# Multiplying the merge gates with the branches' output gates inside the input projection

## The chip, the cores and the metric

The kernel runs on one NeuronCore of a Trainium2 chip. The metric is the device time of one launch in microseconds (us). The engines are named as the profile names them: PE is TensorE (PEld its weight loads), DVE VectorE, ACT ScalarE, POOL GpSimd, SP SyncE, which here only issues DMA transfers.

## What is computed

The network is an attention block of two layers over 1024 tokens of width 1024, and behind it one hybrid block. The change lies in the hybrid block. Cut to what matters there:

```python
proj = h @ w_in                                     # [1024, 14368]
(a_q, a_f, a_i, a_g, b_q, b_k, b_v, b_gk, b_g,
 c_qkv, c_a, c_b, c_g, merge) = jnp.split(proj, cuts, axis=-1)
...
gk  = b_gk @ gla_w_gk + gla_b_gk                    # from 16 columns of proj
y_a = rmsnorm(o_a, hgrn_onorm) * silu(a_g)          # each [1024, 1024]
y_b = rmsnorm(o_b, gla_onorm)  * silu(b_g)
y_c = rmsnorm(o_c, gdn_onorm)  * silu(c_g)
g = sigmoid(merge).reshape(..., 3, 1024)
y = g[:, :, 0] * y_a + g[:, :, 1] * y_b + g[:, :, 2] * y_c
x = x + rmsnorm(y @ w_out, ln_mix_post)
x = x + rmsnorm(square(relu(rmsnorm(x) @ w_up)) @ w_down, ln_mlp_post)
```

The kernel uses sigmoid(m) = (1 + tanh(m/2)) / 2. The factor 1/2 is folded into the head gains `onorm`, so a merge gate enters as 1 + tanh(m/2). Everything is float32.

## The kernel before

The hybrid block is a row of stages, each a block of its own with a barrier of all engines at its end. Four matter here.

**The input projection** is `seven_products`. It first computes one plain product, then the 32 narrow columns (16 of `b_gk`, 16 of `c_a` and `c_b`) into the SBUF tensor `low`, and then 13 groups, q = 0 to 12, of 1024 output columns each. A group is done with seven half-size products (i = 0 to 6) in place of eight. Each product has two units, u = 0 and 1, of 24 times 3 matmul passes over split operands; units are counted g = 0 to 13 within a group below (units 12 and 13 are product 6; "unit 14" is the next group's first, "unit 16" its third). For a unit ACT rounds half a weight block (`unit_hi`, line 900, into `p_th`), DVE forms the rest (`unit_lo`, line 1028, into `p_tl`), and PE waits for the latter. `th` and `tl` have two buffers, so unit g + 2 is prepared after PE has finished unit g. DVE also forms the sums of weight blocks T1 to T4 (lines 1033, 1038, 1042, 1046); T1 of the next group stands ahead of `unit_lo(14)`, T2 ahead of `unit_lo(15)`. The products 2, 4, 5 and 6 give the group's outputs, four tiles of 128 x 512 each: DVE adds PSUM to a partial sum into one of four slots of the ring `stg` (`joined`, lines 1059 and 1061), ACT applies a function in place (`activated`, line 911), in some groups POOL multiplies in place by a head gain (line 979), and SP stores the tile (line 719); `joined` waits until the slot's last store has landed. On ACT and DVE the order is written out: `unit_hi(g + 2)` and `unit_lo(g + 2)`, then the four tiles of `activated` or `joined`.

Groups 4, 8 and 9 are the output gates `b_g`, `c_g` and `a_g`: Silu on ACT, then the gain on POOL. Groups 10 to 12 are the three merge gates: Tanh on ACT, then the store. The result lies in `pn_dram`.

**The small projections** (`small_projections`) multiply `low` with two small matrices on PE right at the block's start. **The branches** (`gated_linear`, `gated_delta`) follow and write their normed outputs to `o_dram[0..2]`.

**The closing stage** (`closing`) merges. For each of eight row tiles SP loads three branches of three 128 x 1024 tiles: output gate `g`, merge gate `mg`, branch output `o`. DVE (`merge`, lines 3564 to 3573) computes (mg + 1) * g, times o, and sums over the branches into `y`; PE turns `y` (line 3322) and multiplies it with `w_out` (line 3327), in plain float32. A tile's loads go into one of two buffers, and SP issues tile t + 2 once `y` of tile t is ready.

Of the kernel before, what the change touches and what calls it, by code (L numbers as in the profile page):

```python
# [20 lines left out]
P = 128  # L21
# [576 lines left out]
def seven_products(C, x_in, first, groups, gains):  # L598
# [7 lines left out]
    with ExitStack() as st:  # L606
# [22 lines left out]
        sq = C.low  # L629
        ps = st.enter_context(nc.psum_tensor("p2_ps", [P, NB, CH], F32))  # L630
# [36 lines left out]
        s_gn = sem("gain_multiplied")  # L667
        block = st.enter_context(nc.Block())
# [10 lines left out]
        for g in groups:  # L679
            n_act.append(n_act[-1] + (16 if g["act"] else 0))  # L680
            n_gain.append(n_gain[-1] + (16 if g["gain"] is not None else 0))
# [9 lines left out]
        def _(sp):  # L691
# [17 lines left out]

            def store(q, i, j):  # L710
                n = out_n(q, i, j)
                k = n - PLAIN - 16 * q
                if groups[q]["gain"] is not None:
                    sp.wait_ge(s_gn, n_gain[q] + k + 1)
                elif groups[q]["act"]:
                    sp.wait_ge(s_act, n_act[q] + k + 1)
                else:
                    sp.wait_ge(s_C, ADDS * q + added[i] + (2 * j if i == 5 else j) + 1)
                sp.dma_start(where(q, i, j), stg[:, n % SG, :]).then_inc(s_st[n % SG], 16)

# [20 lines left out]
            for u in range(NB):  # L741
                store_plain(1, u)
            for q in range(NQ):
                for i, freed in ((2, ((1, 8), (3, 10))), (4, ((0, 12),)), (5, ((2, 14),)), (6, ())):
# [114 lines left out]
        def _(act):  # L859
# [48 lines left out]
            def activated(q, i, j):  # L908
                x = stg[:, out_n(q, i, j) % SG, :]
                act.wait_ge(s_C, ADDS * q + added[i] + (2 * j if i == 5 else j) + 1)  # L910
                act.activation(x, x, groups[q]["act"], scale=0.5 if groups[q]["act"] == ACT.Tanh else 1.0).then_inc(s_act, 1)
# [41 lines left out]
        def _(pool):  # L953
# [996 lines left out]
def small_projections(C):  # L1950
# [4 lines left out]
    with ExitStack() as st:  # L1955
# [8 lines left out]
        s_gD = sem("logits_taken_by_dve")  # L1964
        block = st.enter_context(nc.Block())

        @block.tensor
        def _(pe):
            for h in range(2):
# [1182 lines left out]
def closing(C, out):  # L3152
# [11 lines left out]
    br = [N_AG, N_BG, N_CG]  # L3164
    NJ = len(br)
# [6 lines left out]
    with ExitStack() as st:  # L3172
# [20 lines left out]
        o, g, mg = (lambda b, j, i=i: ogm[:, b, i, j, :] for i in range(3))  # L3193
# [459 lines left out]
def second_block(C, out, x_in):  # L3653
# [5 lines left out]
    with ExitStack() as s2:  # L3659
# [12 lines left out]
        with fresh_semaphores(nc):  # L3672
            with ExitStack() as s3:
                C.spare, C.low = spare, sb("low", [P, SEQ], F32, s3)
                C.onorm = [sb(f"onorm{j}", [P, D // h], F32, s3) for j, h in enumerate((A_HEADS, B_HEADS, C_HEADS))]
                w = ins["w_in_2"][0]
                pt, pn = C.pt_dram, C.pn_dram
                token = lambda a, c, act=None, gain=None: dict(w=w[:, a:a + D], out=pn[:, c:c + D], kind="token", act=act, gain=gain)
                silu = lambda j: dict(act=ACT.Silu, gain=C.onorm[j][:])
                channel = lambda a, r, act=None: dict(w=w[:, a:a + D], out=pt[r:r + D, :], kind="channel", act=act, gain=None)  # L3680
# [4 lines left out]
                               + [token(MERGE + D * i, N_M + D * i, ACT.Tanh) for i in range(3)],  # L3685
# [143 lines left out]
```

## Time and profile before

| | |
|---|---|
| time, median of 3 runs | 4582.42 us (4579.99 to 4585.22) |
| the profiled execution | 4588.66 us, span 4586.9 us |
| granted TensorE clock, mean | 0.965 of full speed |
| PE busy | 4186.2 us, 91% |
| DVE, ACT, POOL busy | 55%, 39%, 14% |
| the 13 groups of the projection | about 1805 to 2822 us of the span |
| small projections | 2825.0 to 2841 us |
| merge and its product | 3730.7 to 3873.5 us |

The span is the time from the first to the last instruction of the profiled execution; its own run took 1.8 us more than the span. Full speed of the clock (1.00) is 2.4 GHz, 0.50 is 1.2 GHz.

### The profile page before, as it was taken

How to read it: one execution, taken by the hardware profiler on the slowest of the kernel's cores; microseconds unless marked ns; L12 is line 12 of the kernel's file. 1: busy time of each engine (PE TensorE's matmuls, PEld its weight loads, DVE VectorE, ACT ScalarE, POOL GpSimd, SP SyncE). 2: the span in 40 equal slices, each digit the busy share in tenths (PEclk: the TensorE clock that was granted, in tenths of full speed). 3: DMA queues.
4: the chain of work that ended last, by engine and by line, in shares of the span. 5: the costliest groups of instructions: out<-in, count | busy, mean ns of one | idle time of the engine just before them, and what ended most of it. 6: DMA issues, size and time to landing. Idle time of an engine off the chain costs nothing. (4 is left out here: it accounts for less than half of the span.)

```text
span 4586.9 us, 66646 instructions
## 1 busy us (share of the span) xinstructions
PE 4186.2 (91%) x26765; PEld 3263.0 (71%) x26765; DVE 2513.5 (55%) x3323; ACT 1799.9 (39%) x3273; POOL 657.2 (14%) x759
## 2 busy tenths in 40 slices
PE   7999889889988979999999997788589979999999
PEld 1887667668756767888887785565388855888887
DVE  1413777651277756555656553787577756334333
ACT  0312456431145642222223333777566513423222
POOL 0200400020030010000102200776212101000000
PEclk9999999999999989999999998899799989999999
DMA  7434411134331131333333232112211056323322
GB/s 268 160 112 155 143 60 49 63 135 142 117 128 55 44 129 56 119 102 103 117 101 120 101 120 78 47 62 89 95 43 39 30 200 236 110 101 129 101 92 83
DMA packets 250802, 485.61 MB, mean 106 GB/s; under 512 B 33048, under 2 KB 73208, under 8 KB 250124
## 3 DMA queue, kind: packets, MB, share of 16 engines
q1 hardware_dynamic: 250512, 481.60, 30.4%
q8 instruction: 199, 3.26, 0.3%
q14 instruction: 91, 0.75, 0.1%
HBM read 360.42 MB, written 121.13 MB: 105 GB/s over the span
## 5 line engine op out<-in xcount | busy, mean ns | idle before, releaser
L1028 DVE TENSOR_TENSOR p_tl<-spare,p_th 128x1024 fp32r<-128x1024 f32 x156 | 199.4, 1279 | 359.4 <-ACT p_th L900 359.4
L900 ACT CAST p_th<-spare 128x1024 fp32r<-128x1024 f32 x156 | 163.5, 1049 | 566.7 <-PE p_ps L852 566.7
L316 PE MATMUL p_ps<-p_wh,hi 128*128 128x512 f32 x896 | 352.2, 393 | 5.7 <-DVE p_wl L484 5.7
L316 PE MATMUL p_ps<-p_wh,lo 128*128 128x512 f32 x896 | 350.2, 391 | 0.0
L316 PE MATMUL p_ps<-p_wl,hi 128*128 128x512 f32 x896 | 350.1, 391 | 0.0
L852 PE MATMUL p_ps<-p_th,p_xh 128*128 128x512 f32 x784 | 310.2, 396 | 2.0 <-DVE p_tl L1028 2.0
L852 PE MATMUL p_ps<-p_th,p_xl 128*128 128x512 f32 x784 | 309.9, 395 | 0.0
L852 PE MATMUL p_ps<-p_tl,p_xh 128*128 128x512 f32 x784 | 309.9, 395 | 0.0
L852 PE MATMUL p_ps<-p_xh,p_th 128*128 128x512 f32 x672 | 263.1, 391 | 1.0 <-DVE p_tl L1028 1.0
L852 PE MATMUL p_ps<-p_xh,p_tl 128*128 128x512 f32 x672 | 263.7, 392 | 0.0
L852 PE MATMUL p_ps<-p_xl,p_th 128*128 128x512 f32 x672 | 262.6, 391 | 0.0
L3594 DVE TENSOR_TENSOR z_wl<-spare,z_wh 128x2048 fp32r<-128x2048 f32 x62 | 142.1, 2293 | 182.1 <-ACT z_wh L3476 182.1
L484 DVE TENSOR_TENSOR p_wl<-p_raw,p_wh 128x2048 fp32r<-128x2048 f32 x40 | 91.5, 2292 | 242.1 <-ACT p_wh L408 242.1
L3345 PE MATMUL z_ps<-z_wh,z_uh 128*128 128x512 f32 x512 | 199.6, 390 | 1.8 <-ACT spare L3483 1.6
L3345 PE MATMUL z_ps<-z_hi,z_wh 128*128 128x512 f32 x512 | 200.0, 391 | 0.0
L3345 PE MATMUL z_ps<-z_hi,z_wl 128*128 128x512 f32 x512 | 199.2, 389 | 0.0
L3345 PE MATMUL z_ps<-z_wh,z_ul 128*128 128x512 f32 x512 | 199.2, 389 | 0.0
L3345 PE MATMUL z_ps<-z_wl,z_uh 128*128 128x512 f32 x512 | 199.2, 389 | 0.0
L3345 PE MATMUL z_ps<-z_lo,z_wh 128*128 128x512 f32 x512 | 199.2, 389 | 0.0
L316 PEld LDWEIGHTS p_ps<-p_wh,hi 128*128 128x128 f32 x896 | 169.3, 189 | 41.1 <-DVE p_wl L484 6.5
L316 PEld LDWEIGHTS p_ps<-p_wl,hi 128*128 128x128 f32 x896 | 169.4, 189 | 34.9
L316 PEld LDWEIGHTS p_ps<-p_wh,lo 128*128 128x128 f32 x896 | 169.1, 189 | 35.4
(422 smaller groups left out, 9902.8 us busy)
## 6 DMA issues: line engine op xcount, KB each, us to landing
spare<-w_in SPq DMA_DIRECT2D x56, 1024.0 KB, 5.6
p_raw<-w_in SPq DMA_DIRECT2D x40, 1024.0 KB, 5.9
pn_dram<-p_stg SPq DMA_DIRECT2D x128, 256.0 KB, 2.0
spare<-w_down SPq DMA_DIRECT2D x32, 1024.0 KB, 4.8
spare<-w_up SPq DMA_DIRECT2D x30, 1024.0 KB, 5.3
p_dram<-p_stg SPq DMA_DIRECT2D x112, 256.0 KB, 2.1
m_w<-w_mod SPq DMA_DIRECT2D x12, 2048.0 KB, 11.8
pt_dram<-p_stg SPq DMA_DIRECT2D x96, 256.0 KB, 2.2
```

Of the source, the lines that this page charges most:

```text
L316: mm = pe.matmul(ps[:, u, :], lhsT, rhs, start=(kk == 0 and q == 0), stop=(kk == KD - 1 and q == 2))
L484: dve.tensor_tensor(wl[:, kh], raw[:, kh], wh[:, kh], ALU.subtract).then_inc(s_wl[kh], 1)
L852: mm = pe.matmul(ps[:, bank + j, :], lhsT, rhs, start=(kk == 0 and e == 0), stop=(kk == KH - 1 and e == 2))
L900: act.copy(th[:, g % 2], (R11, T, R21, R12, R22, R11, R21)[i][:, 2 * u:2 * u + 2]).then_inc(s_hi, 1)
L1028: dve.tensor_tensor(tl[:, g % 2], (R11, T, R21, R12, R22, R11, R21)[i][:, 2 * u:2 * u + 2], th[:, g % 2], ALU.subtract).then_inc(s_lo, 1)
L3345: mm = pe.matmul(ps_ap, lhs[a], rhs[b], start=(start and q == 0), stop=(stop and q == 2))
L3594: dve.tensor_tensor(wl[:, b], raw(b, n), wh[:, b], ALU.subtract).then_inc(s_wl[b], 1)
```

## The change

The multiplication of the two gates moves from the closing stage into groups 10 to 12 of the projection, where the merge gate is made. There, ACT applies Tanh, drains, and adds 1 with a second instruction; POOL multiplies the tile by the output gate, which SP loads back from `pn_dram` (48 loads of 256 KB, three buffers, the first three ahead, each further one after the store of the tile three before it). The buffers are the two halves of `low` and one new tensor `gt`; so SP writes the 32 narrow rows of `low` to DRAM after the narrow product, and the small projections load them back before their first matmul. In the closing stage the load of `g` goes, with the instruction (mg + 1) * g.

```diff
+        gate = (C.low[:, 0:CH], C.low[:, CH:], gt[:])
...
+            def load_gate(m):
+                q, i, j = gated[m]
+                _, a, b = next(o for o in OUTS if o[0] == i)
+                from_q = groups[q]["gate_from"]
+                for x in range(SG):
+                    sp.wait_ge(s_st[x], 16 * ((PLAIN + 16 * (from_q + 1)) // SG))
+                sp.dma_start(gate[m % 3], groups[q]["gate"][(j + 4 * a) * P:(j + 4 * a + 1) * P, b * CH:(b + 1) * CH]).then_inc(s_gl[m % 3], 16)
...
                 sp.dma_start(where(q, i, j), stg[:, n % SG, :]).then_inc(s_st[n % SG], 16)
+                if groups[q]["gate"] is not None:
+                    m = gate_n(q) + k + 3
+                    if m < len(gated):
+                        load_gate(m)
...
+            sp.wait_ge(s_eA, 8 + 2)
+            sp.dma_start(C.low_dram, C.low[0:2 * RANK, :]).then_inc(s_low, 16)
...
-                act.activation(x, x, groups[q]["act"], scale=0.5 if groups[q]["act"] == ACT.Tanh else 1.0).then_inc(s_act, 1)
+                e = act.activation(x, x, groups[q]["act"], scale=0.5 if groups[q]["act"] == ACT.Tanh else 1.0)
+                if groups[q]["gate"] is not None:
+                    act.drain()
+                    e = act.activation(x, x, ACT.Copy, bias=1.0)
+                e.then_inc(s_act, 1)
...
+                elif groups[q]["gate"] is not None:
+                    for k in range(16):
+                        m = gate_n(q) + k
+                        pool.wait_ge(s_act, n_act[q] + k + 1)
+                        pool.wait_ge(s_gl[m % 3], 16 * (m // 3 + 1))
+                        x = stg[:, (PLAIN + k) % SG, :]
+                        pool.tensor_tensor(x, x, gate[m % 3], ALU.mult).then_inc(s_gn, 1)
...
+        @block.sync
+        def _(sp):
+            sp.dma_start(low, C.low_dram).then_inc(s_low, 16)
...
+            pe.wait_ge(s_low, 16)
...
                 for j in range(NJ):
-                    sp.dma_start(g(b, j), C.pn_dram[rows, br[j]:br[j] + D]).then_inc(s_in[j][b], 16)
-                    sp.dma_start(mg(b, j), C.pn_dram[rows, N_M + j * D:N_M + (j + 1) * D]).then_inc(s_in[j][b], 16)
+                    sp.dma_start(g(b, j), C.pn_dram[rows, N_M + j * D:N_M + (j + 1) * D]).then_inc(s_in[j][b], 16)
...
-                    dve.wait_ge(s_in[j][b], 48 * (t // 2 + 1))
-                    dve.scalar_tensor_tensor(g(b, j), mg(b, j), 1.0, g(b, j), ALU.add, ALU.mult)
-                    dve.drain()
+                    dve.wait_ge(s_in[j][b], 32 * (t // 2 + 1))
...
-                               + [token(MERGE + D * i, N_M + D * i, ACT.Tanh) for i in range(3)],
+                               + [dict(token(MERGE + D * i, N_M + D * i, ACT.Tanh), gate=pn[:, c:c + D], gate_from=f) for i, (c, f) in enumerate(((N_AG, 9), (N_BG, 4), (N_CG, 8)))],
```

On ACT, in groups 10 to 12, the four tiles of a product stand between two roundings of weight blocks. Before (the end of group 11's product 4 and what follows it):

```order
L900 CAST p_th<-spare 128x1024 x4
L911 ACTIVATE p_stg<-p_stg 128x512 x4
L900 CAST p_th<-spare 128x1024 x2
L911 ACTIVATE p_stg<-p_stg 128x512 x4
L900 CAST p_th<-spare 128x1024 x2
```

Now, one product of such a group (936 is Tanh, 939 adds 1, 925 is the rounding of a weight block):

```order
L925 CAST p_th<-spare 128x1024 x4
L936 ACTIVATE p_stg<-p_stg 128x512
L939 ACTIVATE p_stg<-p_stg 128x512
L936 ACTIVATE p_stg<-p_stg 128x512
L939 ACTIVATE p_stg<-p_stg 128x512
L936 ACTIVATE p_stg<-p_stg 128x512
L939 ACTIVATE p_stg<-p_stg 128x512
L936 ACTIVATE p_stg<-p_stg 128x512
L939 ACTIVATE p_stg<-p_stg 128x512
```

Eight instructions stand ahead of the next rounding in place of four. On SP, in the same groups, each store is now followed by a load of a gate, and the weight block of the next group stands behind four such pairs (`low` and `p_gt` are gate buffers, `spare` holds the weight blocks):

```order
L734 DMA pn_dram<-p_stg 128x512
L723 DMA low<-pn_dram 128x512
L734 DMA pn_dram<-p_stg 128x512
L723 DMA p_gt<-pn_dram 128x512
L734 DMA pn_dram<-p_stg 128x512
L723 DMA low<-pn_dram 128x512
L734 DMA pn_dram<-p_stg 128x512
L723 DMA low<-pn_dram 128x512
L711 DMA spare<-w_in 128x4x512
```

Before, the same place read:

```order
L719 DMA pn_dram<-p_stg 128x512 x4
L704 DMA spare<-w_in 128x4x512
```

## Rows read from the trace of the kernel before

**Rows 1.** The page, busy time by engine.

```profile
PE 4186.2 (91%) x26765; PEld 3263.0 (71%) x26765; DVE 2513.5 (55%) x3323; ACT 1799.9 (39%) x3273; POOL 657.2 (14%) x759
```

**Rows 2.** Stretches of the merge: PE, PEld, DVE, ACT, POOL busy, clock, DMA share, GB/s.

```profile
3730.00:3752.00 22.00, 2.31 (x9) 1.94 (x10) 12.25 (x10) 1.01 (x1) 0.00 (x0) 0.50 0.94 366
3752.00:3761.00 9.00, 9.00 (x20) 3.86 (x20) 7.35 (x6) 0.00 (x0) 0.00 (x0) 0.79 1.03 410
...
3776.00:3873.50 97.50, 97.50 (x284) 47.41 (x283) 76.42 (x87) 33.41 (x64) 13.11 (x30) 1.00 0.70 274
```

**Rows 3.** PE in order of time at the merge: start, us; idle before in brackets.

```profile
3748.50 1.97 PE L3322 MATMUL z_ps<-ident,z_y 128*128 128x128 f32 x8 [26.97 <-DVE z_y L3573]
3751.66 9.16 PE L3327 MATMUL z_ps<-spare,z_yT 128*128 128x512 f32 x16 [1.19 <-ACT z_yT L3437]
...
3775.27 1.04 PE L3322 MATMUL z_ps<-ident,z_y 128*128 128x128 f32 x8
```

**Rows 4.** SP in order of time, the first load of the merge.

```profile
3730.71 0.34 SPq L3256 DMA_DIRECT2D z_ogm<-pn_dram  x1
```

**Rows 5.** DVE in order of time, the merge of row tile 0 and its end.

```profile
3736.95 1.23 DVE L3564 SCALAR_TENSOR_TENSOR z_ogm<-z_ogm 128x1024 f32<-128x1024 f32 x1 [16.19 <-DMA z_ogm<-oa_dram]
...
3740.78 1.22 DVE L3564 SCALAR_TENSOR_TENSOR z_ogm<-z_ogm 128x1024 f32<-128x1024 f32 x1 [1.31 <-DMA z_ogm<-ob_dram]
...
3747.22 1.23 DVE L3573 TENSOR_TENSOR z_y<-z_y,z_ogm 128x1024 f32<-128x1024 f32 x1
```

**Rows 6.** DVE in order of time, group 11 going over to 12 (Tanh only).

```profile
2738.76 2.28 DVE L1033 TENSOR_TENSOR spare<-spare 128x2048 f32<-128x2048 f32 x1
2740.97 1.22 DVE L1028 TENSOR_TENSOR p_tl<-spare,p_th 128x1024 fp32r<-128x1024 f32 x1
...
2745.86 2.48 DVE L1059 TENSOR_TENSOR p_stg<-p_U,p_ps 128x512 f32<-128x512 f32 x4 [0.16 <-issue]
```

**Rows 7.** ACT in order of time, the same place.

```profile
2742.71 1.05 ACT L900 CAST p_th<-spare 128x1024 fp32r<-128x1024 f32 x1 [2.85 <-PE p_ps L852]
2746.59 2.42 ACT L911 ACTIVATE p_stg<-p_stg 128x512 f32<-128x512 f32 x4 [2.83 <-DVE p_stg L1059]
...
2753.91 1.05 ACT L900 CAST p_th<-p_T 128x1024 fp32r<-128x1024 f32 x1 [3.96 <-PE p_ps L852]
```

**Rows 8.** DVE in order of time, group 9 (Silu, then POOL).

```profile
2568.97 2.09 DVE L1028 TENSOR_TENSOR p_tl<-spare,p_th 128x1024 fp32r<-128x1024 f32 x1 [1.74 <-ACT p_th L900]
...
2583.25 2.30 DVE L1028 TENSOR_TENSOR p_tl<-spare,p_th 128x1024 fp32r<-128x1024 f32 x1
```

**Rows 9.** PE in order of time, group 9 going over to 10.

```profile
2585.61 0.50 PE L852 MATMUL p_ps<-p_th,p_xh 128*128 128x512 f32 x1 [0.95 <-DVE p_tl L1028]
```

**Rows 10.** POOL in order of time, group 9's product 4, first and fourth multiply.

```profile
2566.18 2.54 POOL L979 TENSOR_TENSOR p_stg<-p_stg,onorm 128x512 f32<-128x512 f32 x2 [16.37 <-ACT p_stg L911]
...
2569.93 2.28 POOL L979 TENSOR_TENSOR p_stg<-p_stg,onorm 128x512 f32<-128x512 f32 x1
```

**Rows 11.** ACT in order of time, a drain between two dependent instructions.

```profile
1695.40 1.14 ACT L881 ACTIVATE p_full<-p_ps,mix_scale 128x128 f32<-128x128 f32 x4 [2.95 <-PE p_ps L769]
1696.62 0.62 ACT L884 CAST p_xh<-p_full 128x512 fp32r<-128x512 f32 x1
```

**Rows 12.** ACT and then PE in order of time, end of the projection.

```profile
2813.09 0.63 ACT L911 ACTIVATE p_stg<-p_stg 128x512 f32<-128x512 f32 x1 [2.14 <-DVE p_stg L1059]
...
2821.83 0.63 ACT L911 ACTIVATE p_stg<-p_stg 128x512 f32<-128x512 f32 x1 [0.77 <-DVE p_stg L1059]
...
2825.03 7.16 PE L1974 MATMUL s_pg<-low,wg 16*128 16x512 f32 x8 [3.96 <-PEq L606]
```

**Rows 13.** DMA issues by line: count, KB each, median us to landing.

```profile
pn_dram<-p_stg SPq DMA_DIRECT2D x128, 256.0 KB, 2.0
...
a_mix<-mix_dram SPq DMA_DIRECT2D x18, 256.0 KB, 3.7
...
f_raw<-p_dram SPq DMA_DIRECT2D x2, 256.0 KB, 2.5
```

More of the change, by code:

```diff
@@ L629, in seven_products @@
         sq = C.low
+        gt = sb("gt", [P, CH])
+        gate = (C.low[:, 0:CH], C.low[:, CH:], gt[:])
         ps = st.enter_context(nc.psum_tensor("p2_ps", [P, NB, CH], F32))
@@ L667, in seven_products @@
         s_gn = sem("gain_multiplied")
+        s_low = sem("narrow_stored")
+        s_gl = [sem(f"gate_loaded{b}") for b in range(3)]
         block = st.enter_context(nc.Block())
@@ L680, in seven_products @@
             n_act.append(n_act[-1] + (16 if g["act"] else 0))
-            n_gain.append(n_gain[-1] + (16 if g["gain"] is not None else 0))
+            n_gain.append(n_gain[-1] + (16 if g["gain"] is not None or g["gate"] is not None else 0))
+        gated = [(q, i, j) for q in range(NQ) if groups[q]["gate"] is not None for i, _, _ in OUTS for j in range(4)]
+        gate_n = lambda q: 16 * sum(groups[x]["gate"] is not None for x in range(q))
         def where(q, i, j):
@@ L712, in store @@
                 k = n - PLAIN - 16 * q
-                if groups[q]["gain"] is not None:
+                if groups[q]["gain"] is not None or groups[q]["gate"] is not None:
                     sp.wait_ge(s_gn, n_gain[q] + k + 1)
@@ L742, in _ @@
                 store_plain(1, u)
+            sp.wait_ge(s_eA, 8 + 2)
+            sp.dma_start(C.low_dram, C.low[0:2 * RANK, :]).then_inc(s_low, 16)
             for q in range(NQ):
+                if groups[q]["gate"] is not None and gate_n(q) == 0:
+                    sp.wait_ge(s_low, 16)
+                    for m in range(3):
+                        load_gate(m)
                 for i, freed in ((2, ((1, 8), (3, 10))), (4, ((0, 12),)), (5, ((2, 14),)), (6, ())):
@@ L1964, in small_projections @@
         s_gD = sem("logits_taken_by_dve")
+        s_low = sem("low_loaded")
         block = st.enter_context(nc.Block())
+        @block.sync
+        def _(sp):
+            sp.dma_start(low, C.low_dram).then_inc(s_low, 16)
         @block.tensor
         def _(pe):
+            pe.wait_ge(s_low, 16)
             for h in range(2):
@@ L3163, in closing @@
     nc, ins = C.nc, C.ins
-    br = [N_AG, N_BG, N_CG]
-    NJ = len(br)
+    NJ = 3
     FT = FF // P
@@ L3192, in closing @@
         ms = sbk(st, "ms", [P, TT, 2])
-        o, g, mg = (lambda b, j, i=i: ogm[:, b, i, j, :] for i in range(3))
+        o, g = (lambda b, j, i=i: ogm[:, b, i, j, :] for i in range(2))
         w = C.w_out
@@ L3674, in second_block @@
                 C.spare, C.low = spare, sb("low", [P, SEQ], F32, s3)
+                C.low_dram = nc.dram_tensor("low_dram", (2 * RANK, SEQ), F32, kind="Internal").ap()
                 C.onorm = [sb(f"onorm{j}", [P, D // h], F32, s3) for j, h in enumerate((A_HEADS, B_HEADS, C_HEADS))]
@@ L3677, in second_block @@
                 pt, pn = C.pt_dram, C.pn_dram
-                token = lambda a, c, act=None, gain=None: dict(w=w[:, a:a + D], out=pn[:, c:c + D], kind="token", act=act, gain=gain)
+                token = lambda a, c, act=None, gain=None: dict(w=w[:, a:a + D], out=pn[:, c:c + D], kind="token", act=act, gain=gain, gate=None)
                 silu = lambda j: dict(act=ACT.Silu, gain=C.onorm[j][:])
-                channel = lambda a, r, act=None: dict(w=w[:, a:a + D], out=pt[r:r + D, :], kind="channel", act=act, gain=None)
+                channel = lambda a, r, act=None: dict(w=w[:, a:a + D], out=pt[r:r + D, :], kind="channel", act=act, gain=None, gate=None)
                 seven_products(C, x_in, token(A_I, N_AI),
```

## The prediction, as it was put on record before the changed kernel ran

> **What bounds the kernel now.** I read the busy times first: PE is busy 91% of the span [rows 1], so an edit counts only where PE waits. Next came the stretches of the merge. From 3776 to 3873.5 PE is busy 97.50 of 97.50 us [rows 2]; the merge is bound by PE's plain float32 product, not by loads or DVE. It is bound by loads only ahead of its first matmul: PE sits idle 26.97 us until DVE's `y` of row tile 0 [rows 3], and DVE's first instruction waits 16.19 us for loads, its next branch again 1.31 us [rows 5]. In the projection PE waits for `unit_lo` in three places, about 1 us each, always where a group with a POOL multiply goes over to the next; one of them is shown (0.95 us) [rows 9]. The Tanh groups 10 to 12 go over without a gap.
>
> **Term A, the merge's start.** The first load is issued at 3730.71 [rows 4]. Branch 0 (three loads) is there at 3736.95, branch 1 at 3740.78 [rows 5]: 3.83 us for three loads, 1.28 us each. With two loads per branch they come at 3735.67, 3738.23 and 3740.79. Behind the last stand one multiply and one add (1.23 us each, with drains 2.56 us): `y` at 3743.35. Before, it was at 3747.22 + 1.23 = 3748.45 [rows 5]. That is 5.1 us less. PE's turn of tile 1 needs a `y` that is now ready at about 3751, when the first half product is still running (it took 9.16 us at the clock level of 1.2 GHz and now starts at about 3746.6) [rows 2, 3]. Since PE has no gap behind it, all 5.1 us arrive at the end; and the other 21 loads less and 24 DVE instructions less are worth nothing, because PE's product covers them. Bounds: 4.5 us (if the shorter queue doesn't shorten the first landing in full) to 5.5. If the higher clock came before PE's first product instead of inside it, that product would take some 7 us (between its end, 3760.82, and the turn of tile 2 at 3775.27 lie two more of them and a turn [rows 3]), 2.2 us more gained; nothing speaks for it, as PE's idle time stays above 20 us.
>
> **Term B, `low` back from DRAM.** PE's first small matmul starts at 2825.03, with the block [rows 12]; now it waits for a load issued at that moment. No row shows this load (128 KB in 32 rows). The nearest: a store of 256 KB lands in 2.0 us, loads of 256 KB in 2.5 and, behind others, 3.7 us [rows 13]. I take 2.5, as nothing else is in the queue; bounds 2.0 and 3.7. Nothing hides it: PE, ACT and DVE all wait for this product. The store of `low` is early and behind other stores, free.
>
> **Term C, the projection's end.** After the last matmul each tile used to need add, Tanh (ends at 2822.46) and store (landing about 2824.5), then PE goes on at 2825.03 [rows 12, 13]. Now, per tile, Tanh and the +1: a drain costs 0.08 us (1696.54 to 1696.62) [rows 11], so a pair takes 0.63 + 0.08 + 0.53 = 1.24 us. POOL's multiply takes 1.25 us start to start (two in 2.54) [rows 10]. A gate load goes out after the store of three tiles before, so three multiplies take at least 1.25 + 0.55 (issues) + 2.5 (landing) = 4.3 us. From the first Tanh of product 5 (2813.09): first multiply at about 2814.4, the eighth (product 6's last) at 2824.3 to 2825.5, its end 1.25 later, its store landed at 2827.7 to 2828.8. Against 2824.5 that is 3.2 to 4.3; I take 3.6.
>
> **Term D, PE's waits inside groups 10 to 12.** This is the term that is easily missed, since ACT and POOL are mostly idle there. Where groups go over in Tanh form, PE ends unit 13 at 2742.68 (ACT's waiting rounding starts at 2742.71) and `unit_lo(14)` ends at 2742.19: a slack of 0.5 us [rows 6, 7]. Where POOL multiplies, DVE's subtractions of two SBUF tensors and POOL's multiplies exclude each other: `unit_lo` takes 2.09 and 2.30 us instead of 1.22, while a multiply beside it takes 2.28 instead of 1.25 [rows 6, 8, 10]. That made the 0.95 us of [rows 9]. Now, in the times of [rows 6]: the multiplies of product 5 become ready at about 2736.1, 2737.3, 2738.6 and 2739.8. The third (2738.6 to 2739.85) holds T1 from 2738.76 to 2739.85, T1 ends at 2742.05, the fourth multiply, which asked first, runs to 2743.3, `unit_lo(14)` to 2744.5: PE is 1.8 us late (0.95 if T1 gets ahead, as in group 9). Then T2, `unit_lo(15)` and the adds of product 6 (before at 2745.86, now about 2748.1); four pairs on ACT end at about 2753.8, the rounding for unit 16 at 2754.85, and `unit_lo(16)` at 2756.1 to 2756.4. PE needs it two units after unit 13, 11.2 us by [rows 7] (2753.91 - 2742.71), plus the 1.8: at 2755.7. Late again by 0.5. So 2.3 us for each of two transitions (10 to 11, 11 to 12): 4.6. Products 2 and 4: in group 9 `unit_lo(12)` ended at 2571.06 [rows 8], needed at 2584.66 - 11.2 = 2573.46 [rows 7, 9]; the longer ACT work, 4 x (1.24 - 0.60) = 2.5 us (0.60 is a quarter of 2.42 [rows 7]), eats the whole slack of 2.4. I count 0, but it is on the edge, up to 0.5 us in each of six places. Bounds of D: 1.9 (0.95 twice) to 9.4 (3.2 twice, if a pair costs 1.35, plus 3.0).
>
> The weight blocks don't come late: the next group's block 0 is issued 4 multiplies and 4 gate loads later than before, some 5 us, and T1 needs it 16 us after product 4.
>
> On whether POOL waits out a whole DVE instruction or only shares with it, the rows show 0.87 and 1.08 us of stretch, less than a whole multiply of 1.25 [rows 6, 8]. The Trainium skill ("SBUF — State Buffer", Who interferes with whom) states that an instruction of DVE with two SBUF inputs and one of GpSimd that reads SBUF take a shared port in turns, the later one blocked for the whole of the first. By that rule with the full 1.25 each time, D would be some 0.8 us more; the trace agrees as to the kind. [...]
>
> **Sum.** -5.1 + 2.5 + 3.6 + 4.6 = +5.6 us. The profiled execution took 4588.66 us, of which 1.8 around its span of 4586.9; it would be 4594.3, span 4592.5. It lies 6.2 above the median of 4582.42, so the median becomes 4588.0. What a measurement of this kernel can tell from no change is about 0.2%, 9.2 us: +5.6 is no change by that.
>
> **The rivals.**
> 1. As worked out, +2 to +9.2 us: 0.57.
> 2. The projection hides its part: DVE gets its turns first, D stays at 1.9, C at 3.2, B at 2.0, which gives 7.1 - 5.1 = +2.0; with D = 0 and 5.5 gained at the merge -0.3. For it speaks the 0.5 us of slack; against it group 9's gap, which came with one short ACT instruction per tile less than now. From -2 to +2: 0.18.
> 3. Slower by more than 0.2%: PE waits at products 2 and 4 too. It decides from a pair of 1.35 us on ACT, or from gates that land later than 3 us, since each pushes four tiles past a slack of zero: 9.4 + 4.3 + 3.0 - 5.1 = +11.6, and with late gates up to +16 (4594 to 4598). For it: the slack of products 2 and 4 is used up by my own sum. 0.22.
> 4. Faster by more than 0.2%: the clock rises before PE's first product in the merge and B to D cost nothing. That gives -5.5 - 2.2 = -7.7, which still isn't 9.2; it would take a second stall of PE in the merge that I don't see, and PE's unbroken rows speak against one. 0.03.
>
> **How the numbers follow.** The likeliest is case 1, 4588. The range must leave out no more than 2 in 10: from the middle of case 2 (4581) to the far end of case 3 (4598). Chances: faster 0.03, same 0.75, slower 0.22.
>
> **What the profile after would show.** A: first turn of `y` some 12.7 us after the first load of the merge instead of 17.8, PE without a gap behind it. B: PE's first small matmul waits for a DMA on `low` about 2.5 us. C: last projection matmul to first small matmul 8.5 to 12 us instead of 4. D: two gaps of PE at `p_tl` of 1 to 2 us and two of about 0.5 in groups 10 to 12, none at the products 2 and 4. The prediction is wrong if PE stalls at every output product, if the +1 costs a table load on ACT, or if the merge's gain stays under 4 us.

## The result, and the profile after

The changed kernel takes 4593.88 us (median of 20 executions, 4590.47 to 4601.64) against 4584.04 us before (20, 4579.99 to 4589.59): ratio 1.0022, 95% interval 1.0015 to 1.0029. That is 9.8 us slower, clear of no change, and 0.6 us beyond the far end of the prediction's likeliest case (+2 to +9.2). The profiled execution took 4590.47 us, its span 4588.7.

The page of the changed kernel, busy time by engine, answers to [rows 1]: ACT has 48 instructions more (the +1), POOL 48 more (the multiplies), DVE 24 fewer (the merge), PE the same.

```profile
PE 4181.3 (91%) x26765; PEld 3257.7 (71%) x26765; DVE 2487.8 (54%) x3299; ACT 1826.4 (40%) x3321; POOL 720.9 (16%) x807
```

**The merge's start.** SP's first load, DVE's work on row tile 0 and PE's first turn, each in order of time (answering to [rows 3 to 5]):

```profile
3736.84 0.33 SPq L3297 DMA_DIRECT2D z_ogm<-pn_dram  x1
...
3741.72 1.23 DVE L3607 TENSOR_TENSOR z_y<-z_ogm 128x1024 f32<-128x1024 f32 x1 [14.82 <-DMA z_ogm<-oa_dram]
3744.28 1.22 DVE L3609 TENSOR_TENSOR z_ogm<-z_ogm 128x1024 f32<-128x1024 f32 x1 [1.34 <-DMA z_ogm<-ob_dram]
...
3748.14 1.23 DVE L3611 TENSOR_TENSOR z_y<-z_y,z_ogm 128x1024 f32<-128x1024 f32 x1
...
3749.43 1.97 PE L3362 MATMUL z_ps<-ident,z_y 128*128 128x128 f32 x8 [21.76 <-DVE z_y L3611]
3752.59 10.10 PE L3367 MATMUL z_ps<-spare,z_yT 128*128 128x512 f32 x16 [1.19 <-ACT z_yT L3477]
```

From the first load to the first turn are 12.59 us, where they were 17.79 [rows 3, 4]. Half of the gain is loads: branch 1 is there 7.44 us after the first load instead of 10.07. The other half is VectorE: four instructions stand behind that point instead of six, about 1.3 us each. Branch 2's loads are waited for in neither kernel. PE's first product, though, takes 10.10 us instead of 9.16.

**Inside groups 10 and 11.** PE in order of time, its new waits, then DVE and POOL where group 10 goes over to 11:

```profile
2661.61 0.50 PE L877 MATMUL p_ps<-p_th,p_xh 128*128 128x512 f32 x1 [1.71 <-DVE p_tl L1064]
2673.48 0.50 PE L877 MATMUL p_ps<-p_th,p_xh 128*128 128x512 f32 x1 [0.41 <-DVE p_tl L1064]
...
2742.63 0.50 PE L877 MATMUL p_ps<-p_th,p_xh 128*128 128x512 f32 x1 [1.69 <-DVE p_tl L1064]
```

```profile
2655.99 3.33 DVE L1069 TENSOR_TENSOR spare<-spare 128x2048 f32<-128x2048 f32 x1
2659.24 2.31 DVE L1064 TENSOR_TENSOR p_tl<-spare,p_th 128x1024 fp32r<-128x1024 f32 x1
...
2654.61 2.55 POOL L1015 TENSOR_TENSOR p_stg<-p_stg,low 128x512 f32<-128x512 f32 x2
2658.28 2.19 POOL L1015 TENSOR_TENSOR p_stg<-p_stg,p_gt 128x512 f32<-128x512 f32 x1 [1.11 <-DMA p_gt<-pn_dram]
```

DVE's T1 (L1069) starts at 2655.99 while POOL's multiply runs to 2657.16: 3.33 us instead of 2.28 [rows 6]. POOL's next multiply starts at 2658.28, gets through only after T1's end (2659.32) and finishes at 2660.47. `unit_lo(14)` (L1064), queued behind T1, finishes 1.08 us after that instead of needing 1.22 from 2659.24. PE waits 1.71 us for it. What made that last multiply late was its gate (the wait of 1.11 us for a DMA); its +1 had ended at 2656.93. Between two instructions that exclude each other, read such a row by its end: the recorded time of the second holds its waiting. DVE's additions are not stretched: in the same microseconds they take 0.68 us each.

PE loses more by such a pause than the bracket says. At the second row above the matmul starts 0.80 us after the one before it, where 0.23 is usual, and the next one 0.34 after that: 0.67 us for a bracket of 0.41. (A unit is 24 such matmuls in all, 5.6 us, and not the 24 times 3 of the description above.) At the second transition, group 11 to 12, unit 16 starts 0.3 us late without a bracket of its own.

**The projection's end.** SP, POOL, ACT and PE in order of time, around the last matmul of the projection (which ends at 2833.47 - 11.79 = 2821.68):

```profile
2816.39 1.32 POOL L1015 TENSOR_TENSOR p_stg<-p_stg,p_gt 128x512 f32<-128x512 f32 x1
2818.21 0.32 SPq L723 DMA_DIRECT2D p_gt<-pn_dram  x1
2819.76 1.29 POOL L1015 TENSOR_TENSOR p_stg<-p_stg,low 128x512 f32<-128x512 f32 x1 [0.79 <-DMA low<-pn_dram]
2819.98 0.63 ACT L939 ACTIVATE p_stg<-p_stg 128x512 f32<-128x512 f32 x1
2822.70 1.26 POOL L1015 TENSOR_TENSOR p_stg<-p_stg,p_gt 128x512 f32<-128x512 f32 x1 [1.65 <-ACT p_stg L939]
...
2827.35 1.26 POOL L1015 TENSOR_TENSOR p_stg<-p_stg,p_gt 128x512 f32<-128x512 f32 x1 [0.66 <-DMA p_gt<-pn_dram]
...
2831.14 0.32 SPq L2006 DMA_DIRECT2D low<-low_dram  x1
...
2833.47 7.19 PE L2016 MATMUL s_pg<-low,wg 16*128 16x512 f32 x8 [11.79 <-DMA low<-low_dram]
```

PE idles 11.79 us where it idled 3.96 [rows 12]. The last multiply ends at 2828.61, SP stores it, waits for the store to land, and only then can the small projections begin with their own load of `low`, 2.33 us. The loop of store, gate load and multiply runs in laps of three tiles: its multiplies start at 2816.39, 2822.70 and 2827.35, so its last two laps take 6.31 and 4.65 us. The gates of the two laps landed after 4.3 and 2.7 us. At 2822.70 the profile names ACT as what ended the wait, but that tile's +1 had ended at 2820.61; the gate issued at 2818.21 landed last. DVE too now waits here, for staging buffers that wait for POOL (the last number is the wait):

```profile
2820.61 0.69 DVE L1095 TENSOR_TENSOR p_stg<-p_U,p_ps 128x512 f32<-128x512 f32 x1 [1.37 <-DMA pn_dram<-p_stg]
2823.29 0.69 DVE L1095 TENSOR_TENSOR p_stg<-p_U,p_ps 128x512 f32<-128x512 f32 x1 [2.00 <-DMA pn_dram<-p_stg]
```

The page's DMA issues give the gate loads (count, KB each, median us to landing):

```profile
low<-pn_dram SPq DMA_DIRECT2D x32, 256.0 KB, 3.6
...
p_gt<-pn_dram SPq DMA_DIRECT2D x16, 256.0 KB, 3.9
```

**Where the time stands.** To compare executions I cut each at four places: PE's wait for `p_xl` ahead of the first group (it starts again at 1701.41 before, 1696.70 after), the first small matmul, the merge's first load, the first turn of `y`. What lies ahead of the first cut is untouched by every kernel here, yet that cut falls anywhere from 1695.9 to 1707.3, so a difference of spans says little. A stretch says more, but not to the microsecond: the run of experiment 1, whose projection is that of before, has 1125.60 us in the first stretch of the table (before 1123.62), and the second stretch, which no kernel here changes, takes from 898.80 to 907.20 us in the 14 profiled executions.

| stretch, us | before | after |
| --- | --- | --- |
| projection's groups to first small matmul | 1123.62 | 1136.77 |
| to the merge's first load | 905.68 | 903.37 |
| to the first turn | 17.79 | 12.59 |
| to the end of the span | 838.40 | 839.27 |

A finer cut of the projection is the last of the three old gaps of PE (2585.61 before, 2581.23 after), since only the store of `low` changes ahead of it, and that costs nothing (from the first cut to this gap 884.20 us before, 884.53 after). From there to the first small matmul it was 239.42 us, also in experiment 1, and is 252.24: +12.8. With -5.2 at the merge's start and +0.9 behind it, +8.5 us; the medians say +9.8, with 6.9 to 13.3 inside the interval.

### The profile page after: what moved, and what is told of

It reads as the page before. It is cut to its first block and busy times, and to the rows that moved or that the text cites. A ratio compares the mean times of both kernels' runs of the same rounds, so it can differ in the third digit from the quotient of the medians.

```text
span 4588.7 us, 66917 instructions
## 1 busy us (share of the span) xinstructions
PE 4181.3 (91%) x26765; PEld 3257.7 (71%) x26765; DVE 2487.8 (54%) x3299; ACT 1826.4 (40%) x3321; POOL 720.9 (16%) x807
## 5 line engine op out<-in xcount | busy, mean ns | idle before, releaser
L1064 DVE TENSOR_TENSOR p_tl<-spare,p_th 128x1024 fp32r<-128x1024 f32 x156 | 201.5, 1292 | 360.2 <-ACT p_th L925 360.2
L1008 POOL TENSOR_TENSOR p_stg<-p_stg,onorm 128x512 f32<-128x512 f32 x48 | 75.7, 1609 | 785.1 <-ACT p_stg L936 785.1
```

The costliest lines, as they stand in the source:

```text
L1064: dve.tensor_tensor(tl[:, g % 2], (R11, T, R21, R12, R22, R11, R21)[i][:, 2 * u:2 * u + 2], th[:, g % 2], ALU.subtract).then_inc(s_lo, 1)
```

## The experiments

Each ratio is against the kernel before, measured beside it on the same chip, with its 95% interval. The ratio is not simply the quotient of the two medians, so the two can differ by up to 0.0004. Experiments 1 to 5 leave a part of the calculation out or do one twice, and are there for their times alone; 6 to 12 calculate the same as before.

**1. The closing alone.** The merge groups get no gate, and `low` is neither stored nor loaded back:

```diff
-[dict(token(MERGE + D * i, N_M + D * i, ACT.Tanh), gate=pn[:, c:c + D], gate_from=f) ...]
+[token(MERGE + D * i, N_M + D * i, ACT.Tanh) for i in range(3)]
```

> The change's closing alone: six loads per row tile in the merge and no multiplication of gate by gate on VectorE, while the projection is that of before (no +1, no multiply on GpSimd, no gate loads, no store and reload of low). It leaves out the multiplication by the output gates, and the +1. Theory (the terms add up: A -5.1, B +2.3, C +5.5, D +5.0): the first merge load to the first turn takes 12.6 us instead of 17.8, nothing else moves, and the time is about 5 us below before (ratio 0.9989, 0.9984 to 0.9994). Rival (what the merge gains at its start is given back inside it, by a longer stretch at the low clock or by the output projection meeting another wait): the start is 5 us shorter, merge's first load to the kernel's end is not, and the time is that of before within 1.5 us.

Measured: 4580.8 us, ratio 0.999 (0.9981 to 0.9999), 3.6 us below the 4584.36 of before. First load to first turn 12.69 us, from there to the end 839.13. So the start's 5.1 us are real and 0.7 of them are given back behind it. The place is the clock; stretches from the first turn on, of before and then of the changed kernel (us, busy PE, PEld, DVE, ACT, POOL, then the granted clock, DMA share, GB/s):

```profile
3748.50:3754.50 6.00, 4.81 (x12) 2.89 (x13) 4.54 (x4) 1.01 (x1) 0.00 (x0) 0.50 1.03 410
3754.50:3756.50 2.00, 2.00 (x5) 0.85 (x4) 1.91 (x3) 0.00 (x0) 0.00 (x0) 0.67 1.03 410
```

```profile
3749.40:3755.40 6.00, 4.78 (x12) 2.86 (x13) 4.55 (x4) 1.01 (x1) 0.00 (x0) 0.50 1.03 401
3755.40:3757.40 2.00, 2.00 (x4) 0.89 (x3) 1.57 (x2) 0.00 (x0) 0.00 (x0) 0.50 1.00 365
3757.40:3759.40 2.00, 2.00 (x4) 0.72 (x3) 0.00 (x0) 0.00 (x0) 0.00 (x0) 0.69 1.03 375
```

After the wait PE runs at 0.50 (1.2 GHz). It comes back to full some 7.3 us after the first turn before (a third of the second stretch is at full), and some 9.2 us after it in the changed kernel. Two microseconds more at half speed are one microsecond of product: the 0.9 that the first product takes longer. The length of the wait alone doesn't fix it, though. In the seven executions in which PE waits 21.7 to 21.9 us the clock is back after about 9.1 us; waits of 22.0, 22.2, 22.3 and 22.5 us (experiments 6, 8, 5, 4) were followed by 8.2, 7.9, 8.6 and 7.7, and the three of 27.0 to 27.2 by 7.2 to 7.4. So 0.1 to 0.9 us are given back, and what sets how much stays open.

**2. The projection alone.** The merge is put back to nine loads and a multiplication:

```diff
-                    dve.wait_ge(s_in[j][b], 32 * (t // 2 + 1))
+                    dve.wait_ge(s_in[j][b], 48 * (t // 2 + 1))
+                    dve.scalar_tensor_tensor(g(b, j), mg(b, j), 1.0, g(b, j), ALU.add, ALU.mult)
+                    dve.drain()
```

> The change's projection with the old closing: +1, gate loads and the multiply on GpSimd, the store and the reload of low as in the change, and in the merge the nine loads and the multiplication on VectorE of before. It multiplies by the output gate twice. Theory (terms add up): the costs alone, C 5.5 + B 2.3 + D 5.0 = +12.8 us against before (ratio 1.0028, 1.0022 to 1.0034), with the same PE waits in groups 10 to 12 and the same 11.8 us before the first small matmul as in the change. Rival (some 2 us of the change's loss lie elsewhere, in the merge or in stages that the change does not touch): +10 to +11 with the small projections' end to the merge's first load 2 us shorter again, or +15 and more.

Measured: 4598.95 us (5 executions), ratio 1.0035 (1.0021 to 1.0048), +14.6 for the +12.8 of the theory, which lies inside the interval. From the last old gap to the first small matmul 252.29 us, the same as in the whole change to 0.05 us; first load to first turn 17.79, to the end 838.35, both as before. The split within is a little different (D 5.6, with one wait of 0.38 us behind a product 2, and 11.19 us before the first small matmul). The halves give -3.6 + 14.6 = +11.0 against +9.8, which fits within the intervals. The stretch from the small projections to the merge is 906.19 here and was 903.40 in the run of the closing, whose projection is that of before: the 2.3 us by which the changed kernel's profile was shorter there are the spread of executions, and the rival's hidden 2 us aren't shown.

**3. Without the +1**, and **4. without the multiply's width** (the first of 512 columns only):

```diff
-                if groups[q]["gate"] is not None:
-                    act.drain()
-                    e = act.activation(x, x, ACT.Copy, bias=1.0)
```

```diff
-                        x = stg[:, (PLAIN + k) % SG, :]
-                        pool.tensor_tensor(x, x, gate[m % 3], ALU.mult).then_inc(s_gn, 1)
+                        x = stg[:, (PLAIN + k) % SG, 0:1]
+                        pool.tensor_tensor(x, x, gate[m % 3][:, 0:1], ALU.mult).then_inc(s_gn, 1)
```

> The change without ScalarE's drain and +1 (the product is tanh by gate, without the +1), all else as in the change: GpSimd multiplies, gates are loaded, low is stored and reloaded. Theory (TensorE waits at unit 14 because VectorE's adds are stretched by GpSimd's multiply AND ScalarE's pairs make it late): the two new gaps at unit 14 fall from 1.7 to about 1.0 us, those at unit 16 vanish, D falls from 5.0 to about 2, C falls by 0.7; the time is 3 to 4 us below the change (about 1.0014 of before). Rival 1 (GpSimd's port alone): the gaps stay at 1.7 and D at 5.0. Rival 2 (ScalarE's pairs alone): both gaps vanish, D is 0.

> The change with GpSimd multiplying only the first of each tile's 512 columns: its waits, the gate loads, ScalarE's +1, the store and the reload of low all stay. The output gate is left out of the other 511 columns. Theory (VectorE's adds are stretched by GpSimd's multiply, and the pairs make it worse): without the multiply the gaps at unit 14 are 0.5 us or less, D is at most 1, and the adds and subtractions of group 11 and 12 take what they took in group 9 or less. Rival (the pairs of ScalarE alone make the weights' upper parts late): the gaps at unit 14 stay at 1.5 or more. For C: if the gate loads' landing sets the end of the projection, the last matmul to the last store stays near 6 us although the multiply's 1.27 us is gone; if GpSimd's multiplies set it, it falls to 3 us or less.

Measured: without the +1 4589.99 us, 1.0016 (1.0007 to 1.0025); without the multiply 4588.5 us, 1.001 (1.0001 to 1.0019). Leaving out the +1 was forecast to save 3 to 4 us; it leaves +5.6 by the medians where the change has +9.8. PE's waits without the +1, in order of time:

```profile
2660.46 0.50 PE L877 MATMUL p_ps<-p_th,p_xh 128*128 128x512 f32 x1 [1.01 <-DVE p_tl L1061]
...
2740.12 0.50 PE L877 MATMUL p_ps<-p_th,p_xh 128*128 128x512 f32 x1 [1.00 <-DVE p_tl L1061]
```

From 1.7 to 1.0, and nothing at unit 16, as the theory had it. Both forecasts spoke of VectorE's additions as stretched; the rows show T1 and `unit_lo`. Without the multiply T1 is back at 2.28 us and `unit_lo(14)` at 1.21:

```profile
2662.34 2.28 DVE L1069 TENSOR_TENSOR spare<-spare 128x2048 f32<-128x2048 f32 x1
2664.54 1.21 DVE L1064 TENSOR_TENSOR p_tl<-spare,p_th 128x1024 fp32r<-128x1024 f32 x1
```

PE doesn't wait at unit 14 at all, and once 0.24 us at unit 16. From the last old gap to the projection's last matmul it is 235.46 us before, 240.45 in the change (D = 5.0), 237.99 without the +1 (2.5) and 236.20 without the multiply (0.7). Both causes are needed for the 5.0; POOL's is the one without which there is next to nothing.

At the end PE idles 9.44 us before the first small matmul without the multiply and 10.29 without the +1, where it is 11.79 in the change and 3.96 before. Without the multiply the last store is issued some 4.6 us after the last matmul: neither the 6 of the theory nor the 3 of its rival. The multiply's 1.25 us is a part of that loop, but without it PE still idles 5.5 us more than before, 2.3 of them B, so 3.1 of C are left.

**5. Without the last 13 gate loads.**

```diff
-                    if m < len(gated):
+                    if m < len(gated) - 13:
...
-                        pool.wait_ge(s_gl[m % 3], 16 * (m // 3 + 1))
+                        if m < len(gated) - 13:
+                            pool.wait_ge(s_gl[m % 3], 16 * (m // 3 + 1))
```

> The change without the last 13 gate loads: from the fourth tile of the last group on, GpSimd multiplies by the gates that lie in the three buffers already (so those 13 tiles get other tiles' gates). Theory (C's excess over the 3.6 us forecast is the gate loads' landing of 3.6 to 3.9 us in place of 2.5, behind the stores of the same queue): without loads the last matmul to the last store's issue falls from 6.95 to about 5 us (ScalarE's pairs and the last multiply stay), the first small matmul comes 2 us sooner after the last matmul (9.8 instead of 11.8), D stays at 5.0, and the time is 2 us below the change. Rival (GpSimd's multiplies, stretched by VectorE, and ScalarE's pairs set it, the loads were hidden): last matmul to last store stays at 6.5 us or more.

Measured: 4594.22 us, 1.0012 (1.0003 to 1.0021) of a before of 4588.89. PE's idle time before the first small matmul:

```profile
2840.62 4.63 PE L2017 MATMUL s_pg<-low,wg 16*128 16x512 f32 x5 [8.66 <-DMA low<-low_dram]
```

3.1 us less than the 11.79 of the change (2 were forecast), with all multiplies in place. The last store is issued 2.8 us behind the last matmul, where 5 were forecast, the change has 6.95 and before had 1.42. So the gate loads are the largest part of C: 3.1 us of 5.5 by PE's idle time, 4.1 by the last store. D wasn't 5.0 here but 6.2, for a reason that wasn't in my forecast. DVE, T1 at both transitions:

```profile
2666.91 2.29 DVE L1070 TENSOR_TENSOR spare<-spare 128x2048 f32<-128x2048 f32 x1 [1.80 <-DMA spare<-w_in]
...
2748.35 2.29 DVE L1070 TENSOR_TENSOR spare<-spare 128x2048 f32<-128x2048 f32 x1 [1.37 <-DMA spare<-w_in]
```

T1 waits for the next group's weight block 0. SP issues it behind product 4's stores; before, that was 12.45 us ahead of T1 (2726.31 to 2738.76). In the change those stores wait for POOL and its gate loads, and 6.06 us are left (2730.98 to 2737.04). A block lands in 5.7 us at the median and up to 9.7 in the run of the projection alone. In the profiled execution of the change it came in time; here the two blocks took 7.9 and 7.5 us and it didn't.

**6 to 8. Another place, another form, another order.** Experiment 6 puts the gate and merge groups second to seventh, and loads `low` back inside the projection:

```diff
-                               [channel(A_Q, T_AQ, ACT.Silu), channel(A_F, T_AF), channel(B_Q, T_BQ), token(B_V, N_BV), token(B_G, N_BG, **silu(1))]
...
+                               [channel(A_Q, T_AQ, ACT.Silu), token(B_G, N_BG, **silu(1)), token(C_G, N_CG, **silu(2)), token(A_G, N_AG, **silu(0))]
+                               + [dict(token(MERGE + D * i, N_M + D * i, ACT.Tanh), gate=pn[:, c:c + D], gate_from=f) for i, c, f in ((1, N_BG, 1), (2, N_CG, 2), (0, N_AG, 3))]
+                               + [channel(A_F, T_AF), channel(B_Q, T_BQ), token(B_V, N_BV)]
+                               + [channel(C_QKV + D * i, T_C + D * i) for i in range(3)],
...
+                if q > 0 and groups[q - 1]["gate"] is not None and gate_n(q) == len(gated):
+                    sp.dma_start(C.low[0:2 * RANK, :], C.low_dram).then_inc(s_low, 16)
...
+            sp.wait_ge(s_low, 32)
...
-            sp.dma_start(low, C.low_dram).then_inc(s_low, 16)
```

Experiment 7 adds to it `ACT.Sigmoid` for tanh, drain and +1, and leaves the head gains unhalved. Experiment 8 adds to that DVE's order at a group's end:

```diff
-                elif g % UN == 12 and q + 1 < NQ:
-                    T1(q + 1)
                 elif g % UN == 13 and q + 1 < NQ:
                     T2(q + 1)
                 unit_lo(g + 2)
+                if g % UN == 12 and q + 1 < NQ:
+                    T1(q + 1)
```

> The change with its groups in another order: the three gate groups and the three merge groups come second to seventh, the plain ones last, and low is loaded back inside the projection, behind the last multiplied tile, so that the small projections don't wait for it. Theory (B and C are costs of the place at the projection's end, D is a cost of each gate group's end): B goes to 0, the last matmul to the first small matmul is 4 us or less again, D is paid three times (7.5 us), A stays at 5.2 less 0.9 for the clock; sum +2 to +3 against before (1.0005), 7 below the change. Rival 1 (the gate loads and their waits on the stores' queue hold back the block loads of the next group when six active groups follow each other): new waits of TensorE for DMA in groups 4 to 7, the time at or above the change's. Rival 2 (D is a matter of two chained transitions, paid less when another kind of group follows): sum 0 or below.

> As the run with the groups in another order, and ScalarE takes the sigmoid of the merge gates in one operation in place of tanh of half, drain and +1 (the gates' gains are no longer halved, so the product is the same). Theory (ScalarE's pair makes half of D): TensorE's new waits are 1.0 us per gate group, none at unit 16; D falls to 3 x 1.26 = 3.8 us, the sum is -1.3 us against before (0.9997, 0.999 to 1.0004). Rival (a switch of activation tables at each change of function, or a slower sigmoid than tanh at 0.62 us): D stays above 6, and the time within 1 us of the run before it.

> As the run with sigmoid, and VectorE makes the first unit of the next group before the subtraction of T1 in place of after it, at every group's end. Theory (the waits of 1.0 us at unit 14, of the gate groups and of the three groups with gains, are those of a unit queued behind a T1 that GpSimd's multiply stretches to 3.3 us): all six gaps of 1.0 us go, D is near 0 and the three old gaps of the gain groups too, 5 to 7 us below the run with sigmoid alone, 0.9985 of before. Rival (VectorE is full there, so that unit 15, now behind T1, is late instead): a gap of like size appears one unit later, and the time stays.

Measured, against 4588.89 us of before: 6 took 4589.0 us, 0.9999 (0.999 to 1.0009); 7 took 4584.84 us, 0.9995 (0.9986 to 1.0004); 8 took 4585.88 us, 0.9992 (0.9983 to 1.0001). In 6 the small projections start 3.36 us after the last matmul, B and C are gone, and PE waits 1.7 us at three transitions, as forecast; T1 waits for a weight block once, 0.35 us. The time was forecast at +2 to +3 us; it is +0.1 by the medians, and the interval (-4.6 to +4.1) holds both. In 7 six waits of 1.0 us are left, none at unit 16, and the rival's switch of tables is a single load of 1.28 us in the whole projection, in ScalarE's idle time. In 8 these six are gone as well, and three of 0.6 to 0.7 us stand behind the merge groups. The forecast for 8, 5 to 7 us below 7, wasn't met: its median is 1.0 us above that of 7, and the two intervals cover each other. So B and C were the price of the place, and +1 and T1's place in DVE's queue most of D, by PE's waits; by the times none of the three can be told from before.

**9 and 10. What was VectorE's order worth by itself, and with the pair kept?** 9 is the kernel before with only the last diff; 10 is experiment 6 with it.

> The kernel before with one edit: at a group's end VectorE makes the first unit of the next group ahead of T1, as in the run with sigmoid, other order of groups and this edit. Theory (the three waits of 1.0 us at the starts of groups 5, 9 and 10 are a unit queued behind a stretched T1): the three gaps go, -3 us against before (0.9994, 0.9984 to 1.0003), and what the run with all edits has below it is the closing's. Rival (the gaps move to unit 15): the time of before.

> The other order of groups and VectorE's unit ahead of T1, with ScalarE's tanh, drain and +1 kept. Theory (two causes, each half of D): the waits at unit 14 of the gate groups fall from 1.7 us to 0.7 or less, those at unit 16 (0.4) stay or grow since T2 and the additions now come later and ScalarE's pairs hold the next upper part back; the time lies between the runs with and without the pair, near 0.9995 of before. Rival (ScalarE's pair alone holds unit 14 once T1 is out of the way): waits of 1.5 us and more at unit 14 or 15, no gain over the run with the other order alone.

Measured, against 4585.73 us: 9 took 4582.07 us, 0.9993 (0.9984 to 1.0002); 10 took 4592.18 us, 1.0018 (1.0009 to 1.0027). The 3.7 us of 9 are the 3 of the theory, but the interval reaches from -7.3 to +0.9. In 9 the page shows PE's matmuls on a new unit without any wait left (there were 3.0 us):

```profile
L852 PE MATMUL p_ps<-p_th,p_xh 128*128 128x512 f32 x784 | 309.8, 395 | 0.0
...
L852 PE MATMUL p_ps<-p_xh,p_th 128*128 128x512 f32 x672 | 264.3, 393 | 0.0
```

In 10 the waits only moved. PE in order of time, at units 15 and 16 of one group:

```profile
2282.56 0.50 PE L880 MATMUL p_ps<-p_th,p_xh 128*128 128x512 f32 x1 [0.96 <-DVE p_tl L1067]
...
2290.63 0.50 PE L880 MATMUL p_ps<-p_th,p_xh 128*128 128x512 f32 x1 [2.21 <-DVE p_tl L1067]
```

With four pairs of 1.22 us in ACT's queue ahead of the rounding for unit 16, T1's place can't help: my theory had the direction of the moved waits, and not their size. The time was forecast near 0.9995 of before, 4583.4, and came out 8.8 us above that. Up to the small projections its profiled execution takes 1132.23 us against 1132.45 in 6, so PE's waits cost both the same. By the ratios 10 is slower than 6, each against its own before; the two profiled executions go the other way (4589.49 and 4593.68), so they can't show why, and that stays open.

**11. All edits once more, beside 9. 12. The same with weight blocks 0 and 2 issued ahead of the stores of products 4 and 5 in the merge groups.**

> The version with all edits once more, beside the kernel before with its one edit on the same chip: other order of groups, sigmoid, unit ahead of T1, and the change's closing. Theory: the closing is worth 4.3 us net and the edits cost 1 to 2 of it, so this is 2 to 3 us below the kernel before with the unit ahead of T1, and 4 to 6 below the kernel before (0.9989). Rival (the gain comes from VectorE's order alone): both are alike, within 1 us.

> The version with all edits (other order of groups, sigmoid, unit ahead of T1), and in the three merge groups SP issues the next group's weight blocks 0 and 2 ahead of the stores and gate loads of products 4 and 5 in place of behind them. Theory (the gate loads and GpSimd's waits had pushed block 0's issue from 12.5 us to 6.1 us before T1 reads it, against a landing of 5.7 to 7.9 us; that is on the edge and costs 1 to 2 us in some executions): block 0 is issued 12 us or more before T1 again, and the time is 0 to 2 us below the same version without it (0.999 of before). Rival (the early block loads crowd the gate loads, which then land later than 3.9 us, so that GpSimd's last multiplies meet T1 and T2): the waits at the starts of groups 5 to 7 rise above 0.6 us each, the time is above the version's.

Measured: 11 took 4582.03 us, 0.9994 (0.9984 to 1.0003); 12 took 4580.82 us against 4585.7, 0.9992 (0.9983 to 1.0001). By the medians 9 and 11 are alike to 0.04 us, which is the rival's answer: the gain over before is DVE's order alone. From the first cut to the end 11 is 4.2 us shorter than 9 (2877.65 against 2881.83): 5.4 shorter at the merge's start, 1.0 between small projections and merge, 1.1 longer behind the first turn and 1.1 longer in the projection. That is one execution of each, and stretches that no edit touches differ by as much. An interval of 4 us to either side holds both answers; whether the closing pays at last isn't settled. In 12 block 0 goes out some 18 us ahead of T1 (10.6 in 11), and PE's three waits stay at 0.4 to 0.7 us, so the early loads neither crowd the gates nor bring a gain that can be told. So these runs don't show that block 0's late issue costs time.

## Why the prediction came out as it did

The forecast was 4588.0, a change of +5.6; the time is 4593.88, +9.8 against the before measured beside it. All four terms were found where the prediction put them, and the sum of what they measured is 5.5 + 2.3 + 5.0 - 5.2 = +7.6. The mechanism was right; the term that was mis-sized is C.

- **Term A, right**: -5.2 for -5.1, though not by the path named. The working ended with branch 2's loads and two instructions; what ended last was branch 1's loads and four. In the prediction's own figures both paths come to 12.6 us, since two loads (2.56) take just as long as two instructions, and that is luck. It isn't true that all of it arrives: "all 5.1 us arrive at the end" left out that the low clock then reached 1.9 us further into the product, 0.9 back. The prediction had only looked at the clock as a possible gain.
- **Term B, right**: 2.33 for 2.5. Nothing hid it: PE waited for this load in the changed kernel and in experiments 2 to 5 (2.1 to 2.3 us). Inside the projection it costs nothing (experiment 6).
- **Term C, mis-sized**: 5.5 for 3.6, and outside its own bounds of 3.2 to 4.3, the last store's issue now 6.95 us behind the last matmul (2821.68 to 2828.63) instead of 1.42. The failed input is "+ 2.5 (landing)" in the loop of three multiplies, which made a lap 4.3 us; the last two took 6.31 and 4.65. Gate loads stand in one queue with stores, and land in 3.6 to 3.9 us at the median; rows 13 had that number too, for 256 KB behind others, and I took the one of an empty queue. Experiment 5 takes the loads out and gets 3.1 us back; experiment 4 takes the multiplies' length out and gets 2.4 back.
- **Term D, right in mechanism, near in size**: 5.0 for 4.6. The waits are 1.71 and 0.41 us at the first transition and 1.69 at the second, with unit 16 there 0.3 late, for 1.8 and 0.5 at each. In brackets that is 3.8 us, less than the 4.6; about 0.25 us more for each pause, which the working didn't count, brings the total above it, so the closeness of 5.0 is in part luck. The fourth multiply was also later than the working had it, since it waited for its gate; T1 held it in either case. Experiment 3 removes one cause and leaves 2.5, experiment 4 the other and leaves 0.7. Products 2 and 4 cost nothing, as counted (but for one wait of 0.38 us in experiment 2 and one of 0.35 in 6). The Trainium skill ("SBUF — State Buffer", Who interferes with whom) states that the later instruction is blocked for the whole of the first; the ends of the rows above agree (POOL's multiply ends 1.15 us after T1, `unit_lo(14)` 1.08 us after that multiply, each within 0.15 us of its full length alone). The 0.87 and 1.08 us of stretch, which the prediction set beside it as less than a whole multiply, fit the same lock, met part of the way in.
- **Signs of being wrong that didn't appear**: no table load stands with the +1 in ScalarE's rows of the projection, PE doesn't stall at every output product, and the merge's gain is above 4 us (4.3 net of the clock).
- **A step that was wrong without being a term**: "The weight blocks don't come late". The working put T1 16 us after product 4 and the issue 5 us later; the trace of before gives 12.45 us from block 0's issue to T1, and the change leaves 6.06, 6.4 less. It was late in one of the profiled executions with the gate groups last (experiment 5, 1.80 and 1.37 us) and not in the others, and once by 0.35 us in experiment 6.

Of the 9.8 us, A to D give 7.6 and the clock 0.9. The last 1.3 are less than the interval's half width of 3.2; late weight blocks in some executions are a candidate that was seen in experiment 5 and not shown to be it.

## What to carry to other kernels

Reckon a loop that reuses a buffer through store, load and multiply with the landing time measured behind other transfers (here 3.6 to 3.9 us), not with that of an idle queue (2.5), and place it where more matmuls follow, not at a stage's end where nothing does (experiment 6). Every new wait in front of a store is also a wait in front of each load that the same queue issues behind it: measure the distance from the load's issue to its reader before and after. And before adding GpSimd work to an engine pair that excludes each other, look at what stands first in VectorE's queue: here moving one subtraction behind the urgent one took away three waits of 1.0 us (experiment 9), though neither its gain in time (3.7 us by the medians) nor a difference from the closing's 3.6 is clear of noise.

## What the runs showed of the hardware

- After PE's wait at the merge the granted clock stood at 0.50 (1.2 GHz) and was back at full 7.2 to 9.1 us after the first turn: about 9.1 in seven executions with waits of 21.7 to 21.9 us, 7.7 to 8.6 with waits of 22.0 to 22.5, 7.2 to 7.4 with waits of 27.0 to 27.2. A shorter wait didn't bring the clock back sooner, and the length of the wait alone doesn't explain when it came.
- A DVE subtraction of two SBUF tensors and a POOL multiply ran one after the other: 3.33 us recorded for a 128x2048 subtraction that takes 2.28 alone, 2.31 for one of 128x1024 instead of 1.22, 2.19 for a 128x512 multiply instead of 1.25. DVE's additions of a PSUM tile beside the same multiplies stayed at 0.68.
- A drain and a +1 on a 128x512 tile cost 0.6 us a tile on ACT (start to start of pairs 1.22 to 1.24 us, against 0.61 for the tanh alone). The sigmoid took the same time as the tanh, four in 2.43 us, after one table load of 1.28 us ahead of the first (experiment 7).
- A load of 32 rows, 128 KB, from an otherwise idle queue landed after 2.3 us in the change, 2.0 to 2.3 in experiments 2 to 5. Loads of 256 KB behind stores of the same queue landed after 3.6 and 3.9 us at the median, 2.7 to 4.9 in all.
